# Latent attention: the widest tile first, and the value products of two heads in column halves

## The reference

```python
def mla_attention(h, cos, sin, ...):
    q, k_pe, k_nope, v = ...            # 16 heads, 64 + 32 wide keys, 64 wide values
    s = (einsum("bqhd,bkhd->bhqk", qn, k_nope)
         + einsum("bqhr,bkr->bhqk", qp, k_pe)) * MLA_SCALE
    s = where(kpos[None, :] <= qpos[:, None], s, NEG)     # causal
    p = softmax(s)
    o = einsum("bhqk,bkhd->bqhd", p, v)
    return o.reshape(b, t, 16 * 64) @ w_o
```

## Time and profile before

| | us |
|---|---|
| median of 3 runs (range) | 2408.96 (2407.43 to 2409.32) |
| the profiled execution, its own time | 2405.93 |
| span in the profile | 2404.1 |
| PE busy (TensorE matmul) | 2367.6 (98%) |
| DVE busy (VectorE) | 1229.2 (51%) |
| POOL busy (GpSimd) | 1000.2 (42%) |
| ACT busy (ScalarE) | 946.3 (39%) |

### The profile page before, as it was taken

How to read it: one execution, slowest core, us unless ns; L and a number is a source line. 1 busy time by engine, 2 the same in 40 slices (tenths; PEclk the granted TensorE clock), 3 DMA queues, 4 the chain that set the end, 5 groups by cost and what they waited for, 6 DMA issues and landing times.

```text
span 2404.1 us, 29104 instructions
## 1 busy us (share of the span) xinstructions
PE 2367.6 (98%) x10762; PEld 1871.1 (78%) x10762; DVE 1229.2 (51%) x2034; ACT 946.3 (39%) x1426; POOL 1000.2 (42%) x744
## 2 busy tenths in 40 slices
PE   8999999999999999999999999999999999999999
PEld 6777778878888887857778888887557877888887
DVE  4454545244343337795356544556674334645544
ACT  3355444434222335525434222227676433322222
POOL 4324325224544455626425445544022233454443
PEclk9999999999999999999999999999999999999999
DMA  5212223412332323213223232232002421323231
GB/s 173 88 54 93 90 88 104 158 53 93 106 104 87 105 94 110 95 35 105 70 78 102 88 105 99 93 99 74 19 19 88 158 88 53 114 88 100 92 105 70
DMA packets 170086, 218.69 MB, mean 91 GB/s; under 512 B 6584, under 2 KB 144106, under 8 KB 169974
## 3 DMA queue, kind: packets, MB, share of 16 engines
q1 hardware_dynamic: 168278, 214.59, 27.2%
q10 hardware_dynamic: 1696, 2.61, 0.3%
HBM read 215.05 MB, written 2.12 MB: 90 GB/s over the span
## 4 chain that ended last, share of the span: by engine, by line
PE 91%; DVE 3%; ACT 2%; POOL 1%; issue 1%; DMA 1%; SPq 0%; DVEq 0%; ACTq 0%
PE ps_l L901 78%; PE ps_l L1158 2%; PE ps_l L1050 2%; PE ps_l L1320 2%; POOL w_lo L747 1%; PE ps_s L1303 1%; ACT w_hi L1541 1%; PE ps_s L1407 1%; PE ps_s L1235 1%; PE ps_s L1422 1%; PE ps_s L1200 1%; PE ps_s L1244 0%; PE ps_s L901 0%; PE ps_l L1185 0%; DVE small L2920 0%
## 5 line engine op out<-in xcount | busy, mean ns | idle before, releaser
L747 POOL TENSOR_TENSOR w_lo<-w_raw,w_hi 128x512 fp32r<-128x512 f32 (+1 forms) x740 | 1000.0, 1382 | 1382.6 <-ACT w_hi L1541 1365.6
L901 PE MATMUL ps_l<-a_hi,w_hi 128*128 128x512 f32 x1936 | 762.9, 394 | 3.7 <-POOL w_lo L747 2.7
L901 PE MATMUL ps_l<-a_lo,w_hi 128*128 128x512 f32 x1952 | 758.4, 389 | 0.0
L901 PE MATMUL ps_l<-a_hi,w_lo 128*128 128x512 f32 x1936 | 753.9, 389 | 0.0
L1541 ACT ACTIVATE w_hi<-w_raw 128x2048 fp32r<-128x2048 f32 (+2 forms) x196 | 370.6, 1891 | 600.5 <-PE ps_l L901 575.9
L901 PEld LDWEIGHTS ps_l<-a_hi,w_hi 128*128 128x128 f32 x1936 | 362.8, 187 | 89.3 <-issue 8.9
L901 PEld LDWEIGHTS ps_l<-a_lo,w_hi 128*128 128x128 f32 x1952 | 365.9, 187 | 78.6 <-issue 3.1
L901 PEld LDWEIGHTS ps_l<-a_hi,w_lo 128*128 128x128 f32 x1936 | 362.8, 187 | 76.7
L901 PE MATMUL ps_l<-b_hi,w_hi 128*128 128x512 f32 (+1 forms) x892 | 329.4, 369 | 6.6 <-POOL w_lo L747 3.8
L901 PE MATMUL ps_l<-b_lo,w_hi 128*128 128x512 f32 (+1 forms) x892 | 326.7, 366 | 0.0
L901 PE MATMUL ps_l<-b_hi,w_lo 128*128 128x512 f32 (+1 forms) x892 | 326.7, 366 | 0.0
(11 more groups left out here) (303 smaller groups left out, 2522.5 us busy)
## 6 DMA issues: line engine op xcount, KB each, us to landing
w_raw<-in_ffn_w_up_dram SPq DMA_DIRECT2D x44, 1024.0 KB, 5.0
w_raw<-in_w_dram SPq DMA_DIRECT2D x32, 1024.0 KB, 5.4
w_raw<-in_ffn_w_down_dram SPq DMA_DIRECT2D x22, 1024.0 KB, 4.9
w_raw<-in_w_in_dram SPq DMA_DIRECT2D x20, 1024.0 KB, 5.3
w_raw<-in_xa_wkv_dram SPq DMA_DIRECT2D x16, 1024.0 KB, 5.6
w_raw<-in_w_kv_mem_dram SPq DMA_DIRECT2D x8, 1024.0 KB, 5.7
w_raw<-in_xa_wq_dram SPq DMA_DIRECT2D x8, 1024.0 KB, 5.0
w_raw<-in_xa_wo_dram SPq DMA_DIRECT2D x8, 1024.0 KB, 5.1
```

Source lines behind the costliest of these rows:

```text
L747: e.tensor_tensor(w_lo[:, b % 2, o], w_raw[:, b % 2, o], w_hi[:, b % 2, o].bitcast(F32), ALU.subtract).then_inc(w_lo_made[by], 1)
L901: ins = pe.matmul(o, *((v, w) if swap else (w, v)), start=first and n == 0, stop=last and n == 2)
```

## The change

The latent attention gets its own order. Each head's tiles are taken widest first (3, 2, 1, 0). T is four steps behind S instead of three. V is done once for two heads, four steps after the second head's last T: eight matmul instructions that alternate between output partitions 0 to 63 and 64 to 127 of one bank. ScalarE's high part and VectorE's low part then cover all 128 partitions once for two heads. The turned probabilities lie in three buffers (h mod 3), packed as rows without the masked part; the probabilities themselves lie packed too. VectorE's stream of a step is unchanged: maximum and negative maximum of unit n, then reciprocal and multiplication of unit n - 1.

```diff
+LATENT_ORDER = (3, 2, 1, 0)
+
+def latent_events(heads, lag, wait):
+    ev = []
+    n = heads * TT
+    due = {}
+    for step in range(n + lag + wait + 2):
+        if step < n:
+            ev.append(("S", step // TT, LATENT_ORDER[step % TT]))
+        for kind in "PVO":
+            if (step, kind) in due:
+                ev.append((kind, due[step, kind], 0))
+        if lag <= step < n + lag:
+            h, q = divmod(step - lag, TT)
+            ev.append(("T", h, LATENT_ORDER[q]))
+            if h % 2 and q == TT - 1:
+                due[step + wait, "O"] = due[step + wait, "V"] = h // 2
+                due[step + wait + 1, "P"] = h // 2
     return ev
...
-        attention(f"mla{half}", 8, 3, "a", 1)
+        ev, at = latent_events(8, 4, 4), {}
...
+                    if kind == "T":
+                        claim(pe, L, g)
+                        turns += 1
+                        pe.wait_ge(u_p, U[f"mla{half}"] + turns)
+                        for k in range(i + 1):
+                            ins = turn(bank(L, g)[:, k * P:(k + 1) * P], s_lat(i)[:, k * P:(k + 1) * P])
+                        ins.then_inc(l_full, 1)
+                    if kind == "V":
+                        claim(pe, L, g)
+                        wait_read(pe, L, at["T", 2 * h + 1, LATENT_ORDER[-1]])
+                        for k in range(TT):
+                            for e in (0, 1):
+                                m = 64 * (2 * h + e)
+                                ins = pe.matmul(bank(L, g)[64 * e:64 * e + 64, k * P:T], vh[:, k, m:m + 64],
+                                                pt_lat_row(2 * h + e, k), start=k == 0, stop=k == TT - 1)
+                        ins.then_inc(l_full, 1)
...
-                        if u >= 4:
+                        if h:
                             wait_group(act, L, at["T", h - 1, i])
...
                     if kind == "T":
-                        copy_turned(g, h, i)
+                        wait_group(act, L, g)
+                        if h >= 3:
+                            wait_group(act, L, at["V", (h - 3) // 2, 0])
+                        act.activation(pt_lat(h, i), bank(L, g)[:, 0:n].rearrange("p (k q) -> p k q", q=P), ACT.Copy)\
+                            .then_inc(l_free["a"], 1)
                     if kind == "O":
-                        r = slice(64 * (h % 2), 64 * (h % 2) + 64)
                         wait_group(act, L, g)
-                        act.activation(A_hi[r, 4 * half + h // 2, :], bank(L, g)[r, :], ACT.Copy).then_inc(o_hi, 1)
+                        act.activation(A_hi[:, 4 * half + h, :], bank(L, g)[:, :], ACT.Copy).then_inc(o_hi, 1)
...
+                    if kind == "P":
+                        wait_group(dve, L, g)
+                        dve.wait_ge(o_hi, OH[name] + h + 1)
+                        dve.tensor_tensor(A_lo[:, 4 * half + h, :], bank(L, g)[:, :],
+                                          A_hi[:, 4 * half + h, :].bitcast(F32), ALU.subtract).then_inc(l_free["v"], 1)
```

More of the change, by code:

```diff
@@ L402 @@
 NM = {"diff": 0, "fox": 32, "xa0": 48, "xa1": 64, "mla0": 80, "mla1": 112, "xa2": 144}
-OH = {"diff": 0, "fox": 4, "xa0": 8, "xa1": 16, "mla0": 24, "mla1": 32, "xa2": 40}
+OH = {"diff": 0, "fox": 4, "xa0": 8, "xa1": 16, "mla0": 24, "mla1": 28, "xa2": 32}
 UPB = {"mlp": 0, "ffn0": 32, "ffn1": 54}
@@ L851, in _ @@
             load_range(BB["xo1"] + 2, BB["mla_o"] + 2)
-            wait_group(sp, L, plan.events["mla1"][1]["V", 7, 0])
+            wait_group(sp, L, plan.events["mla1"][1]["V", 3, 0])
             load_mem(2)
@@ L1510, in score @@
                         wait_read(pe, L, L.base[f"uk{half}"] + h // 2)
-                    if h == 0 and i == 0:
+                    if h == 0 and i == LATENT_ORDER[0]:
                         wait_read(pe, L, L.base[f"uk{half}"] + 7)
                     masked_score(g, i, [(qh[0:96, h, i * P:(i + 1) * P], kh[0:96, h, :])])
[L1515 to L1518, removed]
+                ev, at = plan.events[f"mla{half}"]
+                turns = 0
+                for kind, h, i in ev:
+                    g = at[kind, h, i]
+                    if kind == "S":
+                        score(g, h, i)
+                    if kind == "T":
[14 more added lines that the diff above has]
+                        ins.then_inc(l_full, 1)
             def mo_ready(k):
-                wait_read(pe, L, plan.events[f"mla{k // 4}"][1]["V", 2 * (k % 4) + 1, 0])
+                wait_read(pe, L, plan.events[f"mla{k // 4}"][1]["V", k % 4, 0])
             stage("mla_o", xa, nb=2, ready=mo_ready)
@@ L2105, in _ @@
                 ev, at = plan.events[name]
[L2106 removed]
+                scored = 0
                 for kind, h, i in ev:
@@ L2915, in _, with normalise @@
                 at = plan.events[name][1]
[L2917 to L2920, removed]
-                    sync()
[L2922 to L2926, removed]
+                def normalise(u):
+                    h, i = u // TT, LATENT_ORDER[u % TT]
+                    wait_read(dve, S, at["S", h, i])
+                    a = u % 8
+                    step(dve.reciprocal(rl[:, a:a + 1], ls[:, a:a + 1]))
+                    sync()
+                    dve.tensor_scalar(s_lat(i), s_lat(i), rl[:, a:a + 1], None, ALU.mult).then_inc(u_p, 1)
+                scored = 0
+                for kind, h, i in plan.events[name][0]:
+                    g = at[kind, h, i]
+                    if kind == "S":
+                        a = scored % 8
+                        wait_group(dve, S, g)
+                        step(dve.reduce_max(mx[:, a:a + 1], bank(S, g)[:, 0:P * (i + 1)], AX_X))
+                        sync()
+                        dve.tensor_scalar(nm[:, a:a + 1], mx[:, a:a + 1], qcol[:, i:i + 1], -1.0, ALU.mult, ALU.mult)\
+                            .then_inc(u_nm, 1)
+                        scored += 1
+                        if scored > 1:
+                            normalise(scored - 2)
+                        if scored == 8 * TT:
+                            normalise(scored - 1)
+                    if kind == "P":
[3 more added lines that the diff above has]
+                                          A_hi[:, 4 * half + h, :].bitcast(F32), ALU.subtract).then_inc(l_free["v"], 1)
             residual(L.base["mla_o"], 8, between=("mla_o", lambda ns: mem_keys(2, ns)))
```

37 lines of the change are left out of this document (24 added, 13 removed).

## The result

The changed kernel took **2388.31 us**, the median of 4 runs (2387.29 to 2388.84). The kernel before took 2408.59 in the same comparison (4 runs, 2407.43 to 2409.32). The ratio is 0.9916, with a 95% interval of 0.9899 to 0.9933: 20.3 us less, against a forecast of 19.0.

A forecast was written before the change was run, and what follows sets the result against it. TensorE, busy 98% of the span, was taken as the bound. Gains of 9.3 us in mla0 and 9.7 in mla1 made 19.0, so 2408.96 - 19.0 = 2390.0 us, range 2385 to 2397.5.

The forecast's parts named there:

- TensorE sheds one V: Value products of two heads: packed in column halves they cost 2.30 us instead of 4.60; TensorE then needs 9.72 per pair.
- VectorE becomes the bound: Middle of the stage: VectorE needs 10.06 us per two heads against TensorE's 9.72, so the period falls from 12.83 to 10.06.
- VectorE stays fed across a V: Around the value products: next score ready after 4.23 us, VectorE holds 4.7 us of work, cover 0.47, so no idling.
- Ramps: Start of each half to VectorE's last multiplication: ends at 1726.8 in mla0 (slow clock counted) and 1807.7 in mla1.
- Tail: End of either half: last multiplication 0.4 us, then low part, turns, copies and value products 4.15, together 4.55.
- Sums: First score to next product: about 45.8 us in mla0 and 44.9 in mla1; gain 9.3 + 9.7 = 19.0.
- A clock fall more: Rival, chance 0.22: idle TensorE in the tail lowers its clock, costing 3.4 us each; one fall 2393.4, two 2396.8.
- the second: Rival, chance 0.13: VectorE runs dry at each group of value products, 0.8 us each, 5 us less gain: 2395.
- the third (VectorE not the bound): Rival, chance 0.09: VectorE's steps shrink when fed, TensorE binds at 9.72 us per pair, 5 us more gain: 2385.
- Halves that don't run together: Rival, chance 0.03: the value products' column halves don't overlap, 12.0 us per pair against 12.83: about 2405.
- lockstep: Rival, chance 0.03: TensorE has no lead, so scores, VectorE's work and value products add up to 16.8 us per pair: 2437.
- The signs: Expected in the trace: value products about 10.1 us apart, clock 1.00 through both tails, TensorE's holes ending on VectorE's multiplication.

The follow-up runs named there:

- Lag 3: Changed kernel with the turns three steps behind the scores instead of four, widest tile still first: 2395.05 us, ratio 0.9949.
- the old timetable: Changed kernel with tiles 0, 1, 2, 3, turns three steps behind scores, value products three steps behind the last turn, still packed for two heads: 2401.41 us.
- something to do in the tail: Changed kernel with first products of the following stage moved ahead of the last turn and last value products in each half: 2387.53 us, ratio 0.9921.
- halves apart: Changed kernel with the two heads' value products issued one column half after the other instead of alternating: 2401.25 us, ratio 0.9972.
- wait 5: Changed kernel with the value products five steps after the second head's last turn instead of four: 2390.48 us, ratio 0.9931.
- wait 3: Changed kernel with the value products three steps after the second head's last turn instead of four: 2394.23 us, ratio 0.9943.

## Why the prediction was right

- **TensorE sheds one V.** Right: 16 records in 2.37, 2.30 less per pair. TensorE's own need per pair is 9.52, not 9.72 (3.61 us of scores and turns a head, where the reading of the earlier trace rows gave 3.71).
- **VectorE becomes the bound.** Right in kind: it is busy without a hole, the doubled reciprocal comes through in full in the middle, and of the missing one only 0.19 us a pair comes back before TensorE binds. The term was mis-sized by 0.32 us per pair: 9.74 measured, 10.06 predicted. I averaged two heads of a VectorE that still had holes (4.7 a head with 0.66 for a low part); fed without pause it needs 4.57 and 0.60. The V distance before was 12.86 per two heads (half of the 25.71 of the earlier trace rows), so the middle gains 3.1 a pair and not 2.8. The Trainium skill's warning (TensorEngine Tiling (Array Packing), "PSUM Bottleneck"), that packing speeds TensorE and leaves the reading of PSUM as it is, agrees with this trace as far as VectorE now paces the stage, by 0.2 us a pair. But what reads PSUM, the maxima and the low part, is only 2 x 2.06 + 0.60 = 4.7 of the 9.74 us from start to start; the other half works on numbers in SBUF.
- **VectorE stays fed across a V.** Right in effect: no hole in the middle. Lag 3 gives one of 0.67 and the old timetable one of 1.13. But the cover of 0.47 that I worked out isn't there: the score arrives just in time, with 0.26 us from mask product to maximum as in the kernels that wait. My working let TensorE do the turn before the V as soon as that tile's multiplication is done, with 4.7 us of work in VectorE's hand. In the trace that multiplication ends at 1711.32 and the turn starts at 1711.62, since TensorE has 9.52 us of work and 0.21 of bank wait to fit into 9.73, and VectorE's four steps are 4.57. That takes up the cover but for 0.04. So nothing was to spare, and that it sufficed is luck. That the exponential behind a V costs nothing holds for the order 3, 2, 1, 0 alone; with 0, 1, 2, 3 it costs part of 0.57 a pair.
- **Ramps.** The start in mla1 was slower than my terms made it. From the first score to the last multiplication it is 1799.11 - 1758.59 = 40.52 us; my terms with the measured durations in them give 1.2 + 8 x 4.57 + 3 x 0.60 - 0.4 + 0.6 = 39.76. The timeline of VectorE shows the 0.76:

```profile
1761.73 0.16 DVE L2980 RECIPROCAL small<-small 128x1 f32<-128x1 f32 x1 [0.23 <-ACT arena L2180]
1761.93 1.05 DVE L2982 TENSOR_SCALAR arena<-arena,small 128x512 f32<-128x512 f32 x1
...
1763.66 0.66 DVE L2982 TENSOR_SCALAR arena<-arena,small 128x384 f32<-128x384 f32 x1
...
1764.87 0.72 DVE L2982 TENSOR_SCALAR arena<-arena,small 128x256 f32<-128x256 f32 x1
```

  The multiplications take 0.49, 0.42 and 0.35 later, when GpSimd is done: 1.17 us more in three instructions, where I had taken 0.6 for all, and the first row sum is waited for, 0.23. In mla0 the slow clock that I had counted at the start isn't there in this profile (1.00 in 1684 to 1688). The kernel with something to do in the tail has the same program up to there and did have it (granted 0.57 on average in 1686 to 1694): its first V came 17.17 us after the first score instead of 16.23. So its absence gave 0.94 us that the forecast had not counted on.
- **Tail.** Last multiplication to next product: 1799.11 to 1803.69 in mla1, 4.58 against 4.55 predicted. In mla0 it is 1725.97 to 1731.90, 5.93: the same, and 1.35 for a V at low clock.
- **Sums.** mla0 45.64 (45.8 predicted), mla1 45.10 (44.9). They agree better than their parts, and that is luck: in mla0 a VectorE that was 1.5 us ahead of my sum (0.94 of it by the clock at the start) paid for the tail's clock, and in mla1 it paid for the slow start. So the profile gives 9.4 + 9.5 = 18.9 in the two stages, with 18.0 in the span; the runs' medians give 20.3. What is beyond that lies inside the interval of the ratio.
- **Rivals.** "A clock fall more" happened in one tail out of two of the profile, but cost 1.35, not 3.4: only the V stood in it, and the products behind it ran at full clock again. It isn't one fall more, either: the profile before has its fall at the start of mla0 and this one has it in the tail. Lag 3 shows the price of the second; the third (VectorE not the bound) came close, 0.2 us a pair away. Halves that don't run together and lockstep did not occur, and the first of them, made by hand, overlaps by 0.74.
- **The signs.** V starts 9.73 apart instead of about 10.1, for the reason above. Two signs failed: the granted clock was not 1.00 through both tails, and TensorE's hole in the middle still ends on the low part and not on the multiplication, because TensorE never gets so far ahead there that it has to wait for a multiplication.

What stays open is why the clock falls in some tails and not in others. In the changed kernel both tails have the same waits of 1.32 and 0.62, yet one last V takes 3.72 and the other 2.38. The order 0, 1, 2, 3 with lag 4 had longer waits before its last V's (2.01 and 0.78) and kept the full clock through both. The V's that fell took 3.13 to 4.54. Nor does a tail at full clock mean that the fall is spared: in the three kernels whose mla0 tail kept it (halves apart, order 0, 1, 2, 3, and wait 5) the clock fell about 18 us later, behind a wait of 2.0 us for GpSimd's low part, and the stretch between the halves took 28.3 us instead of 26.7. With wait 3 and with the moved products it fell at both places. The changed kernel has the same wait of 2.0 us there and no fall. What decides the place was not tested. No kernel here was faster than the changed one by more than the measurement can tell; the one with the smallest median leaves the normalisation out.

## What to carry to other kernels

When packing takes work from the busiest engine, add up the second one's instructions for the same stretch before pricing the gain, from start to start and from a stretch where it is fed; it is the new pace. See then how far behind the next bound stands: here it was TensorE again, 0.2 us a pair. Then make the balance at the place where the long operation stands: what TensorE has to do from its last free turn to the next score, against the steps that VectorE has in hand. Here that balance forecast the holes of two timetables (0.8 for 0.67, 1.1 to 1.2 for 1.13 us) and explained a third only afterwards (1.98), when the V was put at its real place; for the changed kernel itself it promised a cover that isn't there. Neither half of the change would have done alone: packing on the old timetable gains 6 to 7 us, the new timetable with the halves apart about 6, both together 20. Moving a long operation trades the middle against the tail, so both have to be read.

## What the runs showed of the hardware

- Column halves that are issued one head after the other still overlap a little: 16 records in 3.86 us, where two times 2.30 are 4.60 and alternating takes 2.30.
- TensorE's granted clock fell to 0.50 in mla0's tail, behind a wait of 1.32 us and before the last V began, and was back at 1.00 from 1732 on; a V across such a spell took up to 4.54 instead of 2.37 in other kernels. The same waits in the other half of the same execution did not bring it down. In three other kernels a fall came behind a wait of 2.0 us between the halves instead and cost 1.6 us of products. The Trainium skill (TensorE: Matmul & The Clock Gate, "The HAM clock gate") has the throttled state as the default that activity releases; the levels agree with this trace; why two like tails differ is shown by no run here.
- VectorE's multiplications took up to twice their time while GpSimd worked (1.05 against 0.49 for 128x512), its maxima, which read PSUM, did not (0.55, 0.41 and 0.28 at the same place, as in the middle). No run took GpSimd's work away, so this is a coincidence in time and not a shown cause. GpSimd's work there:

```profile
1760.21 5.24 POOL L793 TENSOR_TENSOR w_lo<-w_raw,w_hi 128x512 fp32r<-128x512 f32 x4 [7.32 <-ACT w_hi L1605]
```

- A low part of 128 partitions takes VectorE as long as one of 64: 0.60 us from start to start for 512 columns either way (1707.32 to 1707.92 after, 1713.87 to 1714.47 before).
